# Gate and up of a feed-forward in seven block products of half the tokens

## The chip, the cores and the metric

The kernel runs on one core of one Trainium2 chip. The metric is the time on the device in microseconds (us), the median of several runs. Before the change it is 3476.19 us (3 runs, 3475.81 to 3477.26). A core has five engines with instruction queues of their own: TensorE (PE; its weight loads are PEld in the profile), VectorE (DVE), ScalarE (ACT), GpSimd (POOL) and SyncE (SP). In this kernel SP issues the weight transfers, and the engines wait for one another on semaphores.

## The reference, cut to what matters

All is float32. There are 512 tokens of width 1024, and six feed-forwards (f0 to f5) among attention and recurrent stages. Each feed-forward is

```python
def swiglu(h, w_gu, w_down):                       # f0, f1
    g, u = jnp.split(h @ w_gu, 2, axis=-1)
    return (jax.nn.silu(g) * u) @ w_down

def swiglu_2(x, w_gate, w_up, w_down):             # f2 to f5
    return (jax.nn.silu(x @ w_gate) * (x @ w_up)) @ w_down
```

with an inner width of 2816. `h @ w` for gate and up is a 512 x 1024 by 1024 x 2816 product each.

## The kernel before, in words

Precision. TensorE multiplies numbers rounded to a shorter float32 format (fp32r). Every operand is therefore split in two parts, a main part (rounded, by ScalarE: `hi`, L1145 to L1152) and a lower part (what the rounding left, by VectorE: `lo`, L1649, or `rest`, L1679), and `mm3` (L625 to L627) makes each product of three matmuls: main x main, main x lower, lower x main.

Weights. `weight_units` lists 1 MB units in the order of use; for a feed-forward these are g0, u0, g1, u1, ... g10, u10 (256 columns of gate or up, all 1024 rows: 8 chunks of 128 rows, k = 0 to 7), then d0, d2, ... d20 (rows of the down projection). SP loads them in that order into `STG`, which has three places (`NSTG`); a load waits until `hi` and `lo` of the unit three before have read the place (L445 to L450). ScalarE and VectorE write both parts into `WR`, with three slots (`NWR`); `hi` waits until TensorE has used the unit three before. `after(name)` on ScalarE and VectorE splits the unit three behind `name`.

Feed-forward. On TensorE, `ffn` (L937) makes 22 features of 128 rows for gate and for up; i counts the 11 blocks of 256 columns. Block 0 goes through `first_feats` (L657), which computes each feature in two halves of 256 tokens while the stage before still delivers tokens; blocks 1 to 10 go through `feat` (L641): 8 chunks k of 3 matmuls over all 512 tokens, into one PSUM bank `P`. ScalarE (L1390) applies SiLU to each gate feature (into `XN`), and VectorE (L1990) multiplies it by the up feature into `ACTS`, a view of `BIG`. `prepare(k)` splits an activation for the down projection: into `RB` for k < 4, else over the tokens `HT`, which are free by then. `out_proj` (L732) makes the down projection in groups of two k. `norm_tile` adds and normalizes, and `turn` transposes the result into `HT`.

Order. Each engine's program is written out in the order of its queue, and an instruction that waits holds up all behind it on its engine. GpSimd loads the gains of the norms into `BC` by its own DMA queue (`gain`), and makes a few lower parts outside the feed-forwards.

## Time and profile before

| what | value |
|---|---|
| median of 3 runs | 3476.19 us (3475.81 to 3477.26) |
| span of the profiled execution | 3473.2 us |
| median less span (start and end around the span, and run to run) | 3.0 us |
| PE busy | 3447.0 us, 99% |
| DVE busy | 1442.7 us, 42% |
| ACT busy | 1184.1 us, 34% |
| POOL busy | 154.3 us, 4% |
| chain that ended last | PE 96%, DVE 2%, ACT 2% |
| HBM read | 320.82 MB, 93 GB/s over the span |

No time of its own is given for the profiled execution beside its span. The busy time of PE counts matmuls from start to a modelled end, and neighbours overlap, so the distance between starts tells more than busy time does. The stage f0 runs from about 432 us (its block 0, halves) over 446.5 us (block 1 begins) and 664 us (last up feature) to about 790 us; the other five feed-forwards repeat it.

### The profile page before, as it was taken

To read this page: it belongs to the slowest core of one execution; us is meant where nothing else is said; L and a number is where in the kernel's file an instruction comes from. 1 tells how busy PE (TensorE), PEld (TensorE's weight loads), DVE (VectorE), ACT (ScalarE), POOL (GpSimd) and SP (SyncE) were. 2 spreads that over 40 slices of the span, in tenths; PEclk is the share of its full clock that TensorE was granted. 3 is DMA by queue.
4 is the path that set the end of the run, shared out by engine and by line. 5 is a ranking of instruction groups with operands and counts; after the bars stand their busy time and mean duration, and the time that the engine had idled before them with its cause. 6 is when DMAs were issued, how large, how long until landed. Compare 5 with 4: busy or idle time off the path is not lost.

```text
span 3473.2 us, 39367 instructions
## 1 busy us (share of the span) xinstructions
PE 3447.0 (99%) x17361; PEld 2904.9 (84%) x17361; DVE 1442.7 (42%) x1555; ACT 1184.1 (34%) x1754; POOL 154.3 (4%) x133
## 2 busy tenths in 40 slices
PE   9999999999999999999999999999999999999999
PEld 7788888888888888888888888888888888888887
DVE  4554523337744333332336554223422355552333
ACT  3343422236734222232224343222322233532222
POOL 2110000000000000000000220000000000410000
PEclk9999999999999999999999999999999999999999
DMA  5224232222342322233222203222322223023221
GB/s 155 86 78 140 72 110 97 97 79 92 121 146 66 105 96 95 94 109 97 97 97 77 80 28 106 97 97 97 101 97 96 98 78 112 25 73 101 95 99 57
DMA packets 246477, 325.49 MB, mean 94 GB/s; under 512 B 19361, under 2 KB 215505, under 8 KB 246306
## 3 DMA queue, kind: packets, MB, share of 16 engines
q1 hardware_dynamic: 241520, 308.38, 27.1%
q0 software_dynamic: 4784, 14.59, 1.3%
q8 instruction: 136, 2.23, 0.3%
q14 instruction: 35, 0.29, 0.0%
q10 hardware_dynamic: 2, 0.00, 0.0%
HBM read 320.82 MB, written 2.10 MB: 93 GB/s over the span
## 4 chain that ended last, share of the span: by engine, by line
PE 96%; DVE 2%; ACT 2%; issue 0%; POOL 0%; DMA 0%; DVEq 0%; ACTq 0%
PE P L625 28%; PE P L627 28%; PE P L626 28%; PE P L630 3%; PE P L804 3%; PE P L779 3%; PE P L906 1%; DVE BIG L1662 1%; DVE WR L1654 0%; PE P L907 0%; ACT WR L1152 0%; DVE HT L1662 0%; PE P L1081 0%; PE P L783 0%; PE P L1064 0%; DVE STAT L1789 0%
## 5 line engine op out<-in xcount | busy, mean ns | idle before, releaser
L1654 DVE TENSOR_TENSOR WR<-STG,WR 128x2048 fp32r<-128x2048 f32 (+3 forms) x292 | 646.8, 2217 | 1297.5 <-ACT WR L1152 1297.3
L625 PE MATMUL P<-HT,WR 128*128 128x512 f32 (+1 forms) x3008 | 1119.6, 372 | 3.8 <-DVE HT L1662 2.7
L626 PE MATMUL P<-HT,WR 128*128 128x512 f32 (+1 forms) x3008 | 1116.7, 371 | 0.0
L627 PE MATMUL P<-HT,WR 128*128 128x512 f32 (+1 forms) x3008 | 1116.5, 371 | 0.0
L1152 ACT CAST WR<-STG 128x2048 fp32r<-128x2048 f32 (+3 forms) x324 | 558.8, 1726 | 1066.0 <-PE P L627 1065.4
L625 PEld LDWEIGHTS P<-HT,WR 128*128 128x128 f32 x3008 | 567.4, 189 | 102.0 <-DVE HT L1662 3.0
L627 PEld LDWEIGHTS P<-HT,WR 128*128 128x128 f32 x3008 | 567.5, 189 | 97.3
L626 PEld LDWEIGHTS P<-HT,WR 128*128 128x128 f32 x3008 | 567.6, 189 | 96.8
L625 PE MATMUL P<-WR,HT 128*128 128x512 f32 (+1 forms) x1344 | 523.9, 390 | 1.6 <-DVE WR L1654 1.4
L627 PE MATMUL P<-WR,HT 128*128 128x512 f32 (+1 forms) x1344 | 520.7, 387 | 0.0
L626 PE MATMUL P<-WR,HT 128*128 128x512 f32 (+1 forms) x1344 | 520.3, 387 | 0.0
L625 PEld LDWEIGHTS P<-WR,HT 128*128 128x128 f32 x1344 | 252.4, 188 | 51.7 <-DVE WR L1654 2.2
L627 PEld LDWEIGHTS P<-WR,HT 128*128 128x128 f32 x1344 | 252.3, 188 | 50.3
L626 PEld LDWEIGHTS P<-WR,HT 128*128 128x128 f32 x1344 | 252.5, 188 | 49.0
L1165 ACT ACTIVATE XN<-P 128x512 f32<-128x512 f32 (+1 forms) x156 | 101.5, 652 | 554.4 <-PE P L627 554.4
L1671 DVE SCALAR_TENSOR_TENSOR BIG<-XN,P 128x512 f32<-128x512 f32 x132 | 90.7, 687 | 341.5 <-PE P L627 341.5
L804 PE MATMUL P<-BIG,XN 128*128 128x96 f32 (+2 forms) x928 | 137.3, 286 | 2.1 <-DVE XN L1674 2.1
L1789 DVE TENSOR_REDUCE STAT<-P 128x1 f32<-128x512 f32 (+4 forms) x142 | 84.0, 592 | 117.6 <-PE P L783 84.0
L1165 ACT ACTIVATE BC<-P,STAT 128x256 f32<-128x256 f32 (+3 forms) x192 | 99.1, 520 | 85.6 <-DVE STAT L1789 85.6
L804 PEld LDWEIGHTS P<-BIG,XN 128*128 128x128 f32 x928 | 119.8, 192 | 5.2 <-DVE XN L1674 3.1
L625 PE MATMUL P<-WR,RB 128*128 128x512 f32 (+1 forms) x352 | 116.8, 345 | 0.0
L627 PE MATMUL P<-WR,RB 128*128 128x512 f32 (+1 forms) x352 | 116.2, 343 | 0.0
(204 smaller groups left out, 2413.5 us busy)
## 6 DMA issues: line engine op xcount, KB each, us to landing
STG<-in_w_ffn_gu_dram SPq DMA_DIRECT2D x44, 1024.0 KB, 5.1
STG<-in_ffn_w_gate_dram SPq DMA_DIRECT2D x44, 1024.0 KB, 5.1
STG<-in_ffn_w_up_dram SPq DMA_DIRECT2D x44, 1024.0 KB, 5.1
STG<-in_ffn_w_down_dram SPq DMA_DIRECT2D x44, 1024.0 KB, 4.9
STG<-in_w_ffn_down_dram SPq DMA_DIRECT2D x22, 1024.0 KB, 4.9
STG<-in_w_xkv_dram SPq DMA_DIRECT2D x16, 1024.0 KB, 5.3
STG<-in_w_in_dram SPq DMA_DIRECT2D x12, 1024.0 KB, 5.2
STG<-in_w_xq_dram SPq DMA_DIRECT2D x8, 1024.0 KB, 5.2
```

Of the source, the lines that this page charges most:

```text
L625: pe.matmul(o, lh, rh, start=first, stop=False)
L626: pe.matmul(o, lh, rl, start=False, stop=False)
L627: return pe.matmul(o, ll, rh, start=False, stop=last)
L630: return pe.transpose(o, i, IDENT[0:n, 0:n])
L779: last = pe.matmul(P[:, b, n * kx:(n + 1) * kx], l, r, start=j == 0, stop=j == len(qk) - 1 and a["diag"] is None)
L804: last = pe.matmul(o, PTB[j0 % NP][:, c:c + 128], c_["v"][n][j], start=j == 0, stop=j == nj - 1)
L906: pe.matmul(both, w[0][:, k, 128 * j:128 * j + 128], MT[:, :, k, :], start=k == 0, stop=False)
L1152: a.copy(main, src).then_inc(ac.sem, ac.up("hi", n, *((part,) if part < of - 1 else ())))
L1165: a.activation(o, i, f, **kw).then_inc(ac.sem, ac.up(*point))
L1654: v.tensor_tensor(rests, src, main.bitcast(F32), ALU.subtract).then_inc(ve.sem, ve.up("lo", n))
L1671: v.scalar_tensor_tensor(out=o, in0=x, scalar=s, in1=y, op0=op0, op1=op1).then_inc(ve.sem, ve.up(*point))
L1789: v.tensor_reduce(STAT[:, 80 + h:80 + h + nh], P[:, where[s, "s", i], 0:nh * kx].rearrange("p (h n) -> p h n", h=nh), AX.X, ALU.max, negat ...
```

## The change

Blocks 2 to 10 (`FIRST`, `LAST`) of every feed-forward are computed by another algorithm. Gate and up of a block, each in two halves of the rows k (0 to 3, 4 to 7), times the tokens in two halves (0 to 255, 256 to 511), is a 2 x 2 by 2 x 2 block product. It is made of seven block products in place of eight, with sums of operands. With g', g'' and u', u'' for the row halves:

- sums of weights, per block: S1 = u' + u'' (GpSimd, into `BC`), S3 = g' - u' (over u' in the stage), S2 = S1 - g' (over g'), S4 = g'' - S2 (over g'') (VectorE).
- sums of tokens, once per feed-forward: T5, T7, T6, T4 (VectorE, eight operations of 1024 wide; then split into main and lower part like the weights).
- products p: 1 = g' with the first tokens, 2 = g'' with the first tokens, 3 = S4, 4 = u'' with T4, 5 = S1 with T5, 6 = S2 with T6, 7 = S3 with T7. Each is 2 x 4 x 3 = 24 matmuls of 256 tokens, of operands of 128 x 1024 in main and lower part.
- Between products the sums in PSUM are read: ScalarE copies them after products 1, 6 and 7 (`kept`) before the next product adds to the same place, VectorE adds the other half (`up`, `gate`), ScalarE applies SiLU to a whole pair, and VectorE multiplies.

In steady state the order on TensorE is (i,6) (i,5) (i,7) (i+1,1) (i,4) (i+1,2) (i,3). `WR` becomes a ring of five half slots (`NFORM`) of formed operands; after product e ends, ScalarE makes the main part for product e+5 and VectorE its lower part. The loads of gate i and up i wait for the lower parts of (i-2,3) and (i-2,4); a fourth stage place is laid over `XN`. The places of the activations for the down projection are renumbered (`slot_pair`, `slot_room`), d0, d2 and d4 are split at new points, and GpSimd loads the gains of the norm behind the feed-forward after the lower part of (10,5), not at its start.

The diff, cut to its core:

```diff
+FIRST, LAST = 2, 10
+def products():
+    order = [(FIRST, 1), (FIRST, 2)]
+    for i in range(FIRST, LAST + 1):
+        order += [(i, 6), (i, 5), (i, 7)] + [(i + 1, 1)] * (i < LAST) + [(i, 4)] + [(i + 1, 2)] * (i < LAST) + [(i, 3)]
+    return order
+NFORM = 5
...
+        def stage_free(n):
...
+            if m is not None and m == 3:
+                return [ve.at(s, "act", 2 * FIRST - 1)]
+            if m is not None and m >= 4:
+                return [ve.at(s, "form", PLACE[i - 2, 3 if part == "g" else 4])]
...
+        def form(s, e):
+            return form_slot(s, (e + 3) % NFORM)
+        def form_free(s, e):
+            return mm.at(s, "form", e - NFORM) if e >= NFORM else mm.at("w", U[s, "g", 0] + (1, 1, 2, 3, 3)[e])
...
GpSimd:
+            def ffn(s):
+                for i in range(FIRST, LAST + 1):
+                    up = U[s, "u", i]
+                    g.wait_ge(*landed[stage_of(up)].at("unit", up))
+                    g.wait_ge(*(ve.at(s, "form", PLACE[i - 2, 5]) if i >= FIRST + 2 else ve.at(s, "T32", 4)))
+                    po.tensor_tensor(BC[:, i % 2, :], staged(up)[:, 0:1024], staged(up)[:, 1024:2048],
+                                     ALU.add).then_inc(pl.sem, pl.up(s, "S1", i))
...
TensorE, ffn:
-                for i in range(11):
+                for i in range(FIRST):
...
+                for e, (i, p) in enumerate(PRODUCTS):
+                    sums, rest = 4 * (i % 2), 4 * (i % 2) + 2
...
+                    if p == 6:
+                        g.wait_ge(*ac.at(s, "kept", i, 1))
+                    if p == 7:
+                        g.wait_ge(*ac.at(s, "kept", i, 6))
+                    if p == 4:
+                        g.wait_ge(*ac.at(s, "kept", i, 7))
+                    if p == 3:
+                        g.wait_ge(*ve.at(s, "up", i))
...
+                    g.wait_ge(*ve.at(s, "form", e))
...
+                        for k in range(4):
+                            lh, ll = (z[:, k, 128 * j:128 * j + 128] for z in w)
+                            pe.matmul(o, lh, x[0][:, k], start=k == 0 and p in (1, 2, 5), stop=False, skip_group_check=True)
+                            pe.matmul(o, lh, x[1][:, k], start=False, stop=False, skip_group_check=True)
+                            last = pe.matmul(o, ll, x[0][:, k], start=False, stop=k == 3, skip_group_check=True)
...
ScalarE, ffn:
+                for e, (i, p) in enumerate(PRODUCTS):
...
+                    if p in (1, 6, 7):
+                        g.wait_ge(*mm.at(s, "form", e))
+                        if p == 7:
+                            g.wait_ge(*ve.at(s, "act", 2 * i - 1))
+                        a.copy(UP2 if p == 7 else pair[:, :, 0:256] if p == 1 else pair[:, :, 256:512], sums).then_inc(
+                            ac.sem, ac.up(s, "kept", i, p))
+                    if e + NFORM < len(PRODUCTS):
+                        main(e + NFORM)
+                    if p == 3:
+                        g.wait_ge(*ve.at(s, "gate", i))
+                        fn(pair, pair, ACT.Silu, s, "silu", i)
...
VectorE, ffn:
+                token_sums()
+                after((s, "g", 0))
...
+                for e, (i, p) in enumerate(PRODUCTS):
...
+                    if p == 7:
+                        g.wait_ge(*mm.at(s, "form", e))
+                        g.wait_ge(*ac.at(s, "kept", i, 7))
+                        tt(UP2, UP2, P[:, others:others + 2, 256:512], ALU.add, s, "up", i)
+                    if p == 3:
+                        g.wait_ge(*mm.at(s, "form", e))
+                        tt(pair, pair, P[:, others:others + 2, :], ALU.add, s, "gate", i)
+                    if e + NFORM < len(PRODUCTS):
+                        rests(e + NFORM)
+                    if p == 3:
+                        g.wait_ge(*ac.at(s, "silu", i))
+                        stt(pair[:, :, 0:256], pair[:, :, 0:256], scale, P[:, sums:sums + 2, 0:256], ALU.mult, ALU.mult)
+                        stt(pair[:, :, 256:512], pair[:, :, 256:512], scale, UP2, ALU.mult, ALU.mult, s, "act", 2 * i)
...
+                        i_, p_ = PRODUCTS[e + NFORM]
+                        if p_ == 1:
+                            s1_s3(i_)
+                        if p_ == 4 and i_ < LAST:
+                            s2(i_ + 1)
+                        if p_ == 3 and i_ < LAST:
+                            s4(i_ + 1)
```

`s1_s3(i)` waits for GpSimd's S1 and makes S3; `s2` and `s4` make S2 and S4; `rests(e)` makes a lower part and `main(e)` a main part.

## Rows read from the trace of the kernel before

**Rows 1.** The page: busy time (share of the span), and the chain by engine.

```profile
PE 3447.0 (99%) x17361; PEld 2904.9 (84%) x17361; DVE 1442.7 (42%) x1555; ACT 1184.1 (34%) x1754; POOL 154.3 (4%) x133
...
PE 96%; DVE 2%; ACT 2%; issue 0%; POOL 0%; DMA 0%; DVEq 0%; ACTq 0%
```

**Rows 2.** Waits of PE: who waited <- for whom: us in total, times, longest.

```profile
PE P L625 <- DVE HT L1662: 2.7, 1, 2.7
```

**Rows 3.** PE in order of time: start us, duration us, line, shape.

```profile
438.07 0.28 PE L625 MATMUL P<-HT,WR 128*128 128x256 f32 x1
438.19 0.28 PE L626 MATMUL P<-HT,WR 128*128 128x256 f32 x1
...
450.46 0.39 PE L625 MATMUL P<-HT,WR 128*128 128x512 f32 x1
450.68 0.39 PE L626 MATMUL P<-HT,WR 128*128 128x512 f32 x1
...
```

**Rows 4.** ACT in order of time: SiLUs behind half-width, then full-width features.

```profile
437.91 0.60 ACT L1165 ACTIVATE XN<-P 128x512 f32<-128x512 f32 x1 [2.01 <-PE P L627]
440.79 0.60 ACT L1165 ACTIVATE XN<-P 128x512 f32<-128x512 f32 x1 [2.28 <-PE P L627]
441.28 1.89 ACT L1152 CAST WR<-STG 128x2048 fp32r<-128x2048 f32 x1
...
452.02 0.60 ACT L1165 ACTIVATE XN<-P 128x512 f32<-128x512 f32 x1 [3.50 <-PE P L627]
457.46 0.60 ACT L1165 ACTIVATE XN<-P 128x512 f32<-128x512 f32 x1 [4.84 <-PE P L627]
```

**Rows 5.** Stretches: length, busy PE, PEld, DVE, ACT, POOL (starts); clock; DMA share, GB/s.

```profile
432.00:446.50 14.50, 14.50 (x123) 14.50 (x122) 6.47 (x5) 6.87 (x7) 0.00 (x0) 1.00 0.38 127
446.50:457.40 10.90, 10.90 (x50) 9.00 (x49) 2.98 (x2) 2.51 (x2) 0.00 (x0) 1.00 0.59 192
```

**Rows 6.** DVE groups by form: busy us, mean ns, idle before.

```profile
L1671 DVE SCALAR_TENSOR_TENSOR BIG<-XN,P 128x512 f32<-128x512 f32 x132 | 90.7, 687 | 341.5 <-PE P L627 341.5
...
L1654 DVE TENSOR_TENSOR WR<-STG,WR 128x1024 fp32r<-128x1024 f32 x10 | 12.2, 1223 | 13.9 <-ACT WR L1152 13.9
```

**Rows 7.** DVE in order of time, in f0 and at the end of n0.

```profile
443.21 2.29 DVE L1654 TENSOR_TENSOR WR<-STG,WR 128x2048 fp32r<-128x2048 f32 x1 [6.28 <-ACT WR L1152]
445.42 0.68 DVE L1671 SCALAR_TENSOR_TENSOR BIG<-XN,P 128x512 f32<-128x512 f32 x1
...
2063.23 0.41 DVE L1662 TENSOR_TENSOR HT<-BIG,HT 128x256 fp32r<-128x256 f32 x1
```

**Rows 8.** ACT groups by form: busy us, mean ns, idle before.

```profile
L1165 ACT ACTIVATE XN<-X 128x1024 f32<-128x1024 f32 x20 | 21.2, 1061 | 24.3 <-DVE X L1662 22.2 <-DMA X<-in_x_dram 1.9
...
L1246 ACT COPY XN<-P 128x512 f32<-128x512 f32 x30 | 17.6, 586 | 22.0 <-PE P L630 20.9 <-DVE HT L1662 0.8
...
L1152 ACT CAST WR<-STG 128x1024 fp32r<-128x1024 f32 x10 | 10.5, 1048 | 0.0
```

**Rows 9.** POOL groups, same columns.

```profile
L507 POOL TENSOR_TENSOR HT<-BIG,HT 96x1024 fp32r<-96x1024 f32 x6 | 14.2, 2363 | 0.5
```

**Rows 10.** DMA: landing times of four weight loads; one busy slice; two loads together.

```profile
DMA to landing us min/median/max: 5.0/5.1/5.6
...
449.00:450.00 1.00, 1.00 (x6) 0.81 (x5) 1.00 (x1) 0.00 (x0) 0.00 (x0) 1.00 0.98 340
...
792.21 0.37 SPq L450 DMA_DIRECT2D STG<-in_c_w_in_dram  x1
...
BC<-in_mem_dram POOLq DMA_DIRECT2D x1, 1024.0 KB, 7.5
```

**Rows 11.** POOL in order of time: a load it issued, and two adds.

```profile
793.62 0.72 POOL L550 DMA_DIRECT2D BC<-in_mem_dram  x1 [363.55 <-DVE XN L1671]
...
2046.03 1.82 POOL L494 TENSOR_TENSOR BIG<-BIG 128x768 f32<-128x768 f32 x1 [1.30 <-DVE BIG L1662]
...
2063.39 1.96 POOL L494 TENSOR_TENSOR BIG<-BIG 128x768 f32<-128x768 f32 x1 [4.07 <-DVE BIG L1662]
```

More of the change, by code:

```diff
@@ L263, in build, with raw, stage_of @@
         U = {u[0]: n for n, u in enumerate(units)}
+        downs = [U[f"f{l}", "d", 0] for l in range(6)]
+        slot_of = lambda n: (n - sum(n >= d for d in downs)) % NWR
+        def raw(n):
+            s, part, i = (*units[n][0], 0)[:3]
+            return 2 * (i - FIRST) + (part == "u") if s[0] == "f" and s != "fox" and part in ("g", "u") and i >= FIRST else None
+        def stage_of(n):
+            m = raw(n)
+            if m is None:
+                return slot_of(n)
+            return NSTG if m % 4 == 3 else slot_of(U[units[n][0][0], "g", 0] + 4 + m % 4)
@@ new lines, in staged @@
+        def staged(n):
+            q = stage_of(n)
+            return XN[:, :, :].rearrange("p a n -> p (a n)") if q == NSTG else STG[:, q, :]
+        def stage_free(n):
+            s, part, i = (*units[n][0], 0)[:3]
+            m = raw(n)
+            if m is not None and m == 3:
+                return [ve.at(s, "act", 2 * FIRST - 1)]
+            if m is not None and m >= 4:
+                return [ve.at(s, "form", PLACE[i - 2, 3 if part == "g" else 4])]
+            if m is not None:
+                n0 = U[s, "g", 0] + 1 + m
+                return [ac.at("hi", n0), low(n0)]
+            if n in downs or n - 1 in downs or n - 2 in downs:
+                s = units[n][0][0]
+                last = ((LAST - 1, 3), (LAST, 3), (LAST, 4))[i // 2]
+                return [ve.at(s, "form", PLACE[last])]
+            return [ac.at("hi", n - NSTG), low(n - NSTG)]
@@ new lines, in slot_free, with form_slot @@
+        def slot_free(n):
+            if n in downs or n - 1 in downs or n - 2 in downs:
+                s, _, k0 = units[n][0]
+                return mm.at(s, "form", len(PRODUCTS) - 1 - (3, 1, 0)[k0 // 2])
+            return mm.at("w", n - NWR)
+        def form_slot(s, h):
+            n0 = U[s, "g", 0]
+            q, half = ((n0 + 2, 0), (n0, 0), (n0, 1), (n0 + 1, 0), (n0 + 1, 1), (n0 + 2, 1))[h]
+            return [WR[:, slot_of(n0 + (q - n0)), z, 1024 * half:1024 * half + 1024] for z in range(2)]
@@ new lines, in ffn @@
+                gate(0)
+                after((s, "g", 0))
+                tokens(5)
+                tokens(6)
+                main(0)
+                main(1)
+                gate(1)
+                tokens(7)
+                main(2)
+                main(3)
+                main(4)
+                tokens(4)
+                for e, (i, p) in enumerate(PRODUCTS):
+                    sums = P[:, 4 * (i % 2):4 * (i % 2) + 2, 0:256]
+                    pair = ACTS[:, 2 * i:2 * i + 2, :]
+                    if p in (1, 6, 7):
[9 more added lines that the diff above has]
+                        fn(pair, pair, ACT.Silu, s, "silu", i)
+                    if (i, p) == (LAST, 2):
+                        for k in range(4):
+                            prepare(k)
+                    if (i, p) == (LAST, 7):
+                        hi(U[s, "d", 0])
+                        for k in range(4, 8):
+                            prepare(k)
@@ new lines, in token_sums @@
+                def token_sums():
+                    first, second, up_first, up_second = T32
+                    g.wait_ge(*ve.now())
+                    quadrant(0, 1)
+                    quadrant(1, 4)
+                    g.wait_ge(*ve.now())
+                    tt(first, second, first, ALU.subtract, s, "T32", 5)
+                    quadrant(3, 3)
+                    g.wait_ge(*ve.now())
+                    tt(second, up_second, second, ALU.subtract, s, "T32", 7)
+                    g.wait_ge(*ve.now())
+                    tt(up_second, up_second, first, ALU.subtract, s, "T32", 6)
+                    quadrant(2, 2)
+                    g.wait_ge(*ve.now())
+                    tt(up_first, up_first, up_second, ALU.subtract, s, "T32", 4)
@@ new lines, in tokens, with s1_s3 @@
+                def tokens(p):
+                    main, rests = tokens_of(s, p)
+                    g.wait_ge(*ac.at(s, "T", p))
+                    rest(rests, T32[{5: 0, 7: 1, 4: 2, 6: 3}[p]], main, s, "T", p)
+                def s1_s3(i):
+                    gate, up = U[s, "g", i], U[s, "u", i]
+                    low_ = staged(up)[:, 0:1024]
+                    g.wait_ge(*landed[stage_of(gate)].at("unit", gate))
+                    g.wait_ge(*pl.at(s, "S1", i))
+                    tt(low_, staged(gate)[:, 0:1024], low_, ALU.subtract, s, "S3", i)
@@ new lines, in rests @@
+                def rests(e):
+                    i, p = PRODUCTS[e]
+                    main, rests_ = form(s, e)
+                    g.wait_ge(*ac.at(s, "form", e))
+                    rest(rests_, weights_of(s, i, p), main, s, "form", e)
+                token_sums()
+                after((s, "g", 0))
+                activated(0)
+                tokens(5)
+                tokens(6)
+                s1_s3(FIRST)
+                rests(0)
+                s2(FIRST)
+                rests(1)
```

190 lines of the change are left out of this document (131 added, 59 removed).

## The prediction

> **What bounds the kernel now.** I read the page first: busy shares and the chain that ended last [rows 1]. TensorE is busy for 99% of the span, 96% of the chain is TensorE, and VectorE and ScalarE are at 42% and 34%. The list of who waited for whom [rows 2] says that none of this is hidden idleness: the longest entry of TensorE's waits is 2.7 us in a span of 3473.2. So a change pays by taking TensorE time away, and costs by whatever it newly makes TensorE wait for. Then TensorE's own order of time [rows 3] gives the price of a matmul as the distance between starts, not as its duration (0.28 and 0.39 us, which overlap). Full-width matmuls (512 tokens) start every 0.227 us, half-width ones (256 tokens) every 0.120 us. The SiLUs that follow the feature groups repeat this over 24 matmuls [rows 4]: 437.91 to 440.79 is 2.88 us for 24 half-width matmuls, 452.02 to 457.46 is 5.44 us for 24 full-width ones. The table of stretches [rows 5] shows the half-width rate held for 14.5 us (123 starts, 118 ns each) at granted clock 1.00, the upper level of 2.4 GHz, and the same clock in the full-width stretch behind it.
>
> **The change: what it takes from TensorE.** One weight block (gate and up, 256 columns each) costs 4 features of 24 full-width matmuls now, 4 x 5.44 = 21.76 us. In seven products it costs 7 x 24 half-width matmuls, 7 x 2.88 = 20.16 us. An eighth of the multiplications goes, but half of that is lost again, because a half-width matmul costs 0.120 and not 0.1135. The difference, 1.60 us, comes 9 times (blocks 2 to 10) in each of 6 feed-forwards: 54 x 1.60 = **86.4 us off**. The order per matmul triple and the kinds of operands are those of the half-width rows, so I take no other price.
>
> The Trainium skill, "TensorE: Matmul & The Clock Gate", section "Back-to-back issue gap", gives the isolated gap as N/2.4 + 2.5 ns. By that a block would cost 96 x 215.8 ns = 20.7 us now and 168 x 109.2 ns = 18.3 us after, 128 us off in all. The trace disagrees (227 and 120 ns), and the row decides.
>
> **What it adds on the other engines, per block.** VectorE: seven lower parts and three sums of weights, ten operations of 1024 at 1.223; the gate sum out of PSUM, 1024 wide, at the same; the up sum and two products of 512 at 0.687 [rows 6]. That is 12.23 + 1.22 + 2.06 = 15.5 us against 2 lower parts of 2.29 [rows 7] and 2 products of 0.687, 5.95 us, now. ScalarE: seven casts of 1024 at 1.048, three copies out of PSUM at 0.586, one SiLU of 1024, for which the nearest row is a 1024 activation at 1.061 [rows 8]: 10.2 us. GpSimd: one sum of 1024, 2.36 us by the nearest row, of 96 partitions [rows 9]. All of these fit beside 20.16 us of TensorE: VectorE 77%, ScalarE 51%, GpSimd 12%. So none is the bound by its sum; what can bind is their order.
>
> **The path through the order.** I walked the queues with these durations, 0.05 us a handoff (a cast ends at 441.28 + 1.89 = 443.17, VectorE starts at 443.21, [rows 4, 7]). VectorE's next instruction starts some 0.07 us before the last one's recorded end (443.21 + 2.29 = 445.50, the next at 445.42, [rows 7]), so a 1024 operation occupies 1.15. Formed weights are five products (14.4 us) deep in the ring, so product e+5 is prepared when e ends, with four products (11.5 us) to do 1.05 + 1.22 us in. That cover is wide. VectorE's work is bunched, though: from the end of product 2 of the next block over products 3, 6 and 5 it has about 9.5 us to do without a gap. In that bunch stands the gate sum, behind which ScalarE, in order, has the SiLU and then the copy of product 6, and product 7 waits for that copy. If the gate sum is about 1 us later than in my walk, TensorE stands.
>
> What can make it late is a loop over two loads. Gate i may land only when the lower part for product 3 of block i-2 is made (the end of that bunch). SP issues gate i and up i one behind the other, each 1 MB. GpSimd adds up i's halves. VectorE's S3, at the head of the next bunch, waits for that sum, and the whole bunch is queued behind it. A load alone lands after 5.1 us [rows 10]. Two in a row do not occur on SP's queue in the steady part. Lower bound: the second MB behind the first at the rate of a busy slice, 1.05 MB at 340 GB/s [rows 10], 3.1 and with ramps 3.15, so 5.1 + 3.15 = 8.25 us. Upper bound: an SP load at 792.2 with a 1 MB load from GpSimd's queue at 793.6 that landed 7.5 later, 8.9 us in all [rows 10, 11]. Loop: 8.25 + 0.05 + 2.37 (GpSimd) + 9.46 (VectorE: lower part, S3, gate sum, lower part, two products, S2, two lower parts) + 0.15 (SP) = **20.28 us** against TensorE's 20.16. That is nearly a tie; a loop of 20.5 or more costs about 7 turns of the excess, less 1 us of slack, per feed-forward.
>
> The loop holds GpSimd and a VectorE operation one after the other. The trace has one place that hints at this: the 768-wide GpSimd add that starts at 2063.39 inside a two-input VectorE operation (2063.23 to 2063.64) takes 1.96, where the one at 2046.03 takes 1.82 [rows 7, 11]. If the two run side by side instead, one operation falls out of the loop and it is 19.1 us, with no cost.
>
> The Trainium skill, "SBUF — State Buffer", section "Who interferes with whom", says that a VectorE instruction with two SBUF inputs and a GpSimd instruction that reads SBUF exclude each other for a whole instruction, whoever starts first. By it the loop is 20.3, without it 19.1; the small lengthening in the row agrees, but is too small to prove a full block.
>
> Cost of the loop: lower end 0 (19.1; nothing waited for now, so no gain to win), upper end 7 x (20.93 - 20.16) - 1 = 4.4 us per feed-forward. I take a loop of 20.5, nearer to SP's own queue than to the mixed pair: 7 x 0.34 - 1 = 1.4 us, **8.4 us in all**.
>
> **The ends of each feed-forward.** Start: eight operations for sums of tokens (9.8 us) stand on VectorE ahead of the lower part of up 1, which was made at 443.2 to 445.5 [rows 7] and is needed at 457.4 [rows 4]; even if all 9.8 add to it, 2 us are left. Up 3 loads only after the activation of block 1; its sum is ready about 9 us into the products, and VectorE's next parts wait behind it, but product (2,4), the first that needs one, starts at 17.3: hidden, with 6 us left. End: in block 10 product 4 follows 7 with no product of a next block between them, so the copy of product 7 is bare: 0.16 until the last matmul has drained (0.28 less 0.12) + 0.59 + 0.1 for two handoffs = 0.85 us, six times, **5.1 us**. The first down units (ready 3 us ahead) and the last activations (2 us ahead) are covered. Moved gain loads on GpSimd's queue come before the down phase, some 100 us before use: nothing. The other stages keep their instructions: nothing. DMA bytes do not change.
>
> **Sum.** 86.4 - 8.4 - 5.1 = 72.9 us. The profiled span 3473.2 becomes 3400.3. The median of the runs, 3476.19, lies 3.0 us above the span (what lies around it, plus run to run, 1.5 us); it is unchanged: **3403 us**.
>
> **Rivals.**
> (a) The loop binds in earnest: second landing at 8.9 and a GpSimd sum lengthened by one VectorE operation beside it to about 2.8, loop 21.3. Loss 7 x 1.14 - 1 = 7 us per feed-forward, 42 us in place of 8.4: 3437. For it: a loop without slack, a price of GpSimd known only beside idle VectorE. Against it: the SP queue's landings are even (5.0 to 5.6, [rows 10]).
> (b) Slower than before: the GpSimd sum falls into VectorE's bunch, they stop each other, and the sum takes 5.5 us. The loop is then 23.4, the loss 7 x 3.25 - 1 = 21.8 and 0.9 at the end, against 14.4 won per feed-forward: +8.3 x 6 = 50, 3526. The point from which it decides: a loop of 22.2 us, which is a GpSimd sum of 4.3 us. Against it: the only lengthening seen is 0.14. The Trainium skill names the mechanism ("SBUF — State Buffer", section "Who interferes with whom": "the other fully blocks"), not such a duration.
> (c) The loop does not bind, 19.1 to 20.3, nothing but 5.1 is lost: 3395.
> (d) It does not do what it says: half-width matmuls with a wait every 24 run at the rate per column of full ones or worse. At 0.1295 us each a block costs 21.76 and all is gone: 3482. The rows speak against it [rows 3 to 5], since groups of 24 with waits between them already keep 2.88.
>
> **Chances.** Forecast (3398 to 3412) 0.46; (c) 0.20; (a), from 3412 to 3465, 0.22; (b) 0.06, (d) and a loop that eats just the gain 0.06, two thirds of it within 0.2%. 0.2% (7 us) is about what a measurement of this kernel can tell from no change. Faster by more: 0.88; within: 0.04; slower: 0.08. Range: 3390 (rival (c) with the 5.1 not all bare) to 3445 (rival (a) with a bit more); what lies outside is (b), (d) and the far part of (a), under 0.2.
>
> **What would show it.** Product groups at 2.88 us, seven to a block, show the first step; anything longer at granted clock 1.00 refutes it. TensorE's waits should be on ScalarE's copies: six of 0.85 before product 4 of block 10, and small ones before product 7 of a block, fewer than 0.4 each. The distance between issues of gate loads shows the loop: 20.2 to 20.5. GpSimd's sum at 2.4 shows that the exclusion is cheap, at 3 or over it is rival (a), at 4.3 or over (b). Landing of the up load more than 8.5 after the gate issue also goes to (a). The prediction is wrong if TensorE waits for formed weights, or if the ends of the feed-forwards show waits that I held for hidden.

## The result, and the profile after

The changed kernel takes 3396.94 us (median of 4 runs, 3395.53 to 3397.53) beside 3476.65 us for the kernel before on the same chip: a ratio of 0.9771, 95% interval 0.9757 to 0.9784, 79.7 us less. The forecast was 3403 in a range of 3390 to 3445. The profiled execution has a span of 3395.7 us, the granted clock is 1.00.

The page of the changed kernel: busy time, the chain that ended last, and three groups (busy us, mean ns, idle before), to be read beside [rows 1, 6, 8].

```profile
span 3395.7 us, 48396 instructions
PE 3364.8 (99%) x21249; PEld 3021.7 (89%) x21249; DVE 2048.6 (60%) x2167; ACT 1465.9 (43%) x2156; POOL 299.9 (9%) x187
...
PE 90%; DVE 4%; issue 3%; ACT 2%; POOL 1%; DMA 1%; SPq 0%; DVEq 0%; ACTq 0%; POOLq 0%
...
L1096 PE MATMUL P<-HT,WR 128*128 128x256 f32 x1728 | 489.6, 283 | 4.1 <-ACT CUM L1595 4.1
...
L1851 DVE TENSOR_TENSOR WR<-STG,WR 128x1024 fp32r<-128x1024 f32 x276 | 378.3, 1384 | 112.8 <-ACT WR L1574 112.6
...
L1574 ACT CAST WR<-STG 128x1024 fp32r<-128x1024 f32 x276 | 287.7, 1050 | 204.9 <-PE P L1098 186.4
```

TensorE has 3888 more matmuls and is still busy for 99%. VectorE went from 1442.7 to 2048.6 us, ScalarE from 1184.1 to 1465.9, GpSimd from 154.3 to 299.9, and none of them is near the span. The casts cost what they were priced at (1050 ns), but the 276 of the 378 lower parts in the group shown average 1384 ns and not 1223: the first hint that something stretches VectorE's operations.

TensorE's waits in the changed kernel (who <- for whom: us in total, times, longest), beside [rows 2]:

```profile
PE P L1096 <- ACT CUM L1595: 4.1, 6, 0.7
PE P L748 <- DVE XN L1860: 3.1, 2, 1.6
```

The first entry is new, one in each feed-forward: the copy after product 7 of block 10. In order of time (start us, duration us, and in brackets the idle time before and its cause), the copy and the matmuls behind it:

```profile
645.92 0.59 ACT L1595 COPY CUM<-P 128x512 f32<-128x512 f32 x1 [4.05 <-PE P L1098]
```

```profile
646.56 0.39 PE L1096 MATMUL P<-HT,WR 128*128 128x256 f32 x1 [0.68 <-ACT CUM L1595]
646.78 0.28 PE L1097 MATMUL P<-HT,WR 128*128 128x256 f32 x1
```

The start before 646.56 is 0.96 us earlier, 0.84 more than the usual 0.12, and the next one follows after 0.22 in place of 0.12: 0.93 us in all, before rounding.

I measured the stretch of the 63 products in each feed-forward as the distance from its first matmul's start to its last (1512 starts), and 0.12 us for the last matmul itself. Without a wait it would be 63 x 2.88 = 181.44 us.

| feed-forward | stretch, us | over 181.44 | made of |
|---|---|---|---|
| f0, f1, f4, f5 | 182.37 each (f4, f5 182.36) | 0.93 | the copy after product 7 |
| f2 | 182.72 | 1.28 | the same, and one wait of 0.35 at 1656.20 |
| f3 | 183.42 | 1.98 | the same, and three of 0.35 at 2151.43, 2212.25, 2273.08 |

The sum is 6.96 us: 5.6 for the copies, 1.4 for the four small waits, all four before a product 7. So 54 x 1.60 - 6.96 = 79.4 us should be gained, and 79.7 was by the medians. (The two profiled spans differ by 77.5; the changed kernel's is of the slowest of its four runs.) That leaves the four small waits to explain, and the loop, which was forecast at 8.4 and cost 1.4.

The turn of the loop (from one issue of a gate load to the next) before the wait at 2151.43, in the changed kernel: POOL's sum, then VectorE, then ScalarE.

```profile
2143.90 3.45 POOL L664 TENSOR_TENSOR BC<-STG 128x1024 f32<-128x1024 f32 x1 [15.25 <-DMA STG<-in_ffn_w_up_dram]
```

```profile
2143.86 1.23 DVE L1851 TENSOR_TENSOR WR<-STG,WR 128x1024 fp32r<-128x1024 f32 x1 [1.71 <-ACT WR L1574]
2147.45 1.23 DVE L1851 TENSOR_TENSOR STG<-STG 128x1024 f32<-128x1024 f32 x1 [2.36 <-POOL BC L664]
2148.59 1.21 DVE L1851 TENSOR_TENSOR BIG<-BIG,P 128x1024 f32<-128x1024 f32 x1
```

```profile
2149.84 1.06 ACT L1313 ACTIVATE BIG<-BIG 128x1024 f32<-128x1024 f32 x1 [3.13 <-DVE BIG L1851]
2150.81 0.57 ACT L1595 COPY BIG<-P 128x512 f32<-128x512 f32 x1
```

The sum starts 0.04 us behind a VectorE lower part, and takes 3.45 us where 42 of the 54 sums take 2.39 to 2.42. VectorE stands for 2.36 us on it; S3, the gate sum, the SiLU and the copy of product 6 follow without a gap, the copy ends at 2151.38, and product 7 starts at 2151.43. This is the path that the prediction drew, with a sum 1.05 longer.

In the next turn it is the other way round. SP's gate loads, POOL's sum, then VectorE's lower part and S3:

```profile
2155.66 0.37 SPq L560 DMA_DIRECT2D STG<-in_ffn_w_gate_dram  x1
2175.46 0.37 SPq L560 DMA_DIRECT2D STG<-in_ffn_w_gate_dram  x1
```

```profile
2163.86 2.40 POOL L664 TENSOR_TENSOR BC<-XN 128x1024 f32<-128x1024 f32 x1 [16.52 <-DMA XN<-in_ffn_w_up_dram]
```

```profile
2164.37 2.98 DVE L1851 TENSOR_TENSOR WR<-STG,WR 128x1024 fp32r<-128x1024 f32 x1 [1.71 <-ACT WR L1574]
2167.27 1.21 DVE L1851 TENSOR_TENSOR XN<-STG,XN 128x1024 f32<-128x1024 f32 x1
```

The sum is first and keeps its 2.40 us (to 2166.26). The lower part, begun 0.51 us behind it, takes 2.98 us and ends 1.09 behind the sum's end, so S3 starts 1.01 behind it in place of the 0.10 above. Of the 42 turns (blocks 4 to 10 of six feed-forwards) 38 go like this one. In the other four the sum is stretched, and these are the four before the small waits; the up load had landed late in all of them, 9.29 to 9.61 us after the gate issue.

From one gate issue to the next it is 19.72 to 21.33 us, 20.24 on average over 36 distances. Each is the landing of the up load (7.95 to 9.67 us after the gate issue, in 13 of the 42 turns 9.22 or more) plus 11.65 to 12.05. So a turn with a late landing is longer than TensorE's 20.16, most of the others are shorter, and the lead that is lost in one (how far the copy of product 6 is ready ahead of product 7) is won back in the next. Why every third landing or so is late, no run here shows. Product 7 starts 3.98 us behind the start of S3 where it waits, and 4.11 to 5.74 behind it in the 38 turns where it does not.

### The profile page after: what moved, and what is told of

The parts are those of the page before. It is cut to its first block, busy times and chain, and to the rows that moved or that the text cites. A ratio compares the mean times of both kernels' runs of the same rounds, so it can differ in the third digit from the quotient of the medians.

```text
span 3395.7 us, 48396 instructions
## 1 busy us (share of the span) xinstructions
PE 3364.8 (99%) x21249; PEld 3021.7 (89%) x21249; DVE 2048.6 (60%) x2167; ACT 1465.9 (43%) x2156; POOL 299.9 (9%) x187
## 3 DMA queue, kind: packets, MB, share of 16 engines
q8 instruction: 167, 2.74, 0.3%
## 4 chain that ended last, share of the span: by engine, by line
PE 90%; DVE 4%; issue 3%; ACT 2%; POOL 1%; DMA 1%; SPq 0%; DVEq 0%; ACTq 0%; POOLq 0%
PE P L743 17%; PE P L745 17%; PE P L744 17%; PE P L1096 9%; PE P L1098 9%; PE P L1097 9%; PE P L921 3%; PE P L748 3%; PE P L896 3%; DVE BIG L1851 1%; PE P L1023 1%; POOL BC L664 1%; DMA STG<-in_ffn_w_up_dram 1%; DVE WR L1843 1%; PE P L1024 0%
## 5 line engine op out<-in xcount | busy, mean ns | idle before, releaser
L1843 DVE TENSOR_TENSOR WR<-STG,WR 128x2048 fp32r<-128x2048 f32 (+3 forms) x184 | 398.5, 2172 | 643.0 <-ACT WR L1300 642.8
L1300 ACT CAST WR<-STG 128x2048 fp32r<-128x2048 f32 (+4 forms) x216 | 352.4, 1637 | 564.6 <-PE P L745 563.8
L1096 PE MATMUL P<-HT,WR 128*128 128x256 f32 x1728 | 489.6, 283 | 4.1 <-ACT CUM L1595 4.1
L1098 PE MATMUL P<-HT,WR 128*128 128x256 f32 x1728 | 489.1, 283 | 0.0
L1097 PE MATMUL P<-HT,WR 128*128 128x256 f32 x1728 | 489.0, 283 | 0.0
L743 PE MATMUL P<-WR,HT 128*128 128x512 f32 (+1 forms) x1248 | 485.7, 389 | 1.6 <-DVE WR L1843 1.4
L745 PE MATMUL P<-WR,HT 128*128 128x512 f32 (+1 forms) x1248 | 483.3, 387 | 0.0
L744 PE MATMUL P<-WR,HT 128*128 128x512 f32 (+1 forms) x1248 | 483.0, 387 | 0.0
L743 PE MATMUL P<-HT,WR 128*128 128x512 f32 (+1 forms) x1280 | 447.8, 350 | 2.7 <-DVE HT L1851 1.6
L1851 DVE TENSOR_TENSOR WR<-STG,WR 128x1024 fp32r<-128x1024 f32 x276 | 378.3, 1384 | 112.8 <-ACT WR L1574 112.6
L744 PE MATMUL P<-HT,WR 128*128 128x512 f32 (+1 forms) x1280 | 444.9, 348 | 0.0
L745 PE MATMUL P<-HT,WR 128*128 128x512 f32 (+1 forms) x1280 | 444.7, 347 | 0.0
L1574 ACT CAST WR<-STG 128x1024 fp32r<-128x1024 f32 x276 | 287.7, 1050 | 204.9 <-PE P L1098 186.4
L1096 PEld LDWEIGHTS P<-HT,WR 128*128 128x128 f32 x1728 | 331.7, 192 | 5.5 <-ACT CUM L1595 5.3
L1097 PEld LDWEIGHTS P<-HT,WR 128*128 128x128 f32 x1728 | 331.7, 192 | 0.2
L1098 PEld LDWEIGHTS P<-HT,WR 128*128 128x128 f32 x1728 | 331.7, 192 | 0.0
L743 PEld LDWEIGHTS P<-WR,HT 128*128 128x128 f32 x1248 | 234.3, 188 | 48.0 <-DVE WR L1843 2.2
L745 PEld LDWEIGHTS P<-WR,HT 128*128 128x128 f32 x1248 | 234.2, 188 | 46.7
L744 PEld LDWEIGHTS P<-WR,HT 128*128 128x128 f32 x1248 | 234.4, 188 | 45.4
L743 PEld LDWEIGHTS P<-HT,WR 128*128 128x128 f32 x1280 | 243.4, 190 | 33.7 <-DVE WR L1843 2.1
L745 PEld LDWEIGHTS P<-HT,WR 128*128 128x128 f32 x1280 | 243.4, 190 | 30.1
L744 PEld LDWEIGHTS P<-HT,WR 128*128 128x128 f32 x1280 | 243.5, 190 | 29.4
```

Source lines behind the costliest of these rows:

```text
L743: pe.matmul(o, lh, rh, start=first, stop=False)
L744: pe.matmul(o, lh, rl, start=False, stop=False)
L745: return pe.matmul(o, ll, rh, start=False, stop=last)
L1096: pe.matmul(o, lh, x[0][:, k], start=k == 0 and p in (1, 2, 5), stop=False, skip_group_check=True)
L1097: pe.matmul(o, lh, x[1][:, k], start=False, stop=False, skip_group_check=True)
L1098: last = pe.matmul(o, ll, x[0][:, k], start=False, stop=k == 3, skip_group_check=True)
```

## The experiments

All times are medians; every kernel but two starts from the changed one (3396.9 us). The kernel before took 3476.65 us beside the changed one and 3475.69 to 3476.05 beside the others, so differences under 1 us in the third column say nothing; the last column, from the traces, is the sharper one.

| kernel | us | against the changed one | product stretches over 181.44 us, six together |
|---|---|---|---|
| changed | 3396.9 | | 7.0 |
| sum on VectorE | 3394.8 | -2.1 | 5.6 |
| up load first | 3394.7 | -2.3 | 5.6 |
| last block reordered | 3392.4 | -4.6 | 2.4 |
| up load first, last block reordered | 3389.1 | -7.9 | 0.0 |
| sum twice | 3510.6 | +113.7 | 120.1 |
| sum twice, up load first | 3396.3 | -0.7 | 6.6 |
| zeros ahead of the sum | 3420.4 | +23.5 | 29.0 |
| before, half-width features | 3544.7 | (before: 3476.1) | |
| before, quarter-width features | 4616.8 | (before: 3475.7) | |

### The sum on VectorE

```diff
 GpSimd, ffn:
-                    po.tensor_tensor(BC[:, i % 2, :], staged(up)[:, 0:1024], staged(up)[:, 1024:2048],
-                                     ALU.add).then_inc(pl.sem, pl.up(s, "S1", i))
 VectorE, s1_s3:
+                    g.wait_ge(*landed[stage_of(up)].at("unit", up))
+                    tt(BC[:, i % 2, :], low_, staged(up)[:, 1024:2048], ALU.add, s, "S1", i)
```

> The sum S1 = u' + u'' is made by VectorE, just ahead of S3, and GpSimd makes none. Nothing else changes. My theory: the loop over the two loads does not bind in the changed kernel (7 loads in a row are 20.2 us apart, TensorE's period is 20.16), and its four single waits of 0.35 us before product 7 (one in f2, three in f3) come from a GpSimd sum that VectorE's two-input operation stretched to 3.0 to 3.4 us. Then the sum costs 1.15 us on VectorE in place of 2.41 on GpSimd, the loop gets shorter by 1.2 us (to about 18.9), the four waits go, and the time is 3396.9 - 1.4 = 3395.5 (3394.5 to 3397). Rival: what sets product 7's cover is the length of VectorE's bunch (S3, gate sum, lower parts), 9.5 us now and 10.6 with the sum in it; then the copy before product 7 comes late in every block, 54 waits of 0.3 to 1 us, 3413 to 3450.

3394.81 us (3394.13 to 3396.44; ratio to before 0.9767, 0.9753 to 0.9782). All six stretches are 182.37 us: the four waits of 0.35 are gone, only the copies are left, and the 1.15 us more in VectorE's bunch shows nowhere. The rival falls. The runs alone scarcely tell the two kernels apart; of the 2.1 us between the medians 1.4 are in the stretches, and the kernel before was 0.8 us faster beside this one.

### The up load first

```diff
 SyncE:
+            sequence = list(range(len(units)))
+            for n in range(len(units)):
+                m = raw(n)
+                if m is not None and m >= 4 and m % 2 == 0:
+                    sequence[n], sequence[n + 1] = n + 1, n
-            for n, (_, srcs, p, k, w) in enumerate(units):
+            for n in sequence:
```

> For blocks 4 to 10 SP issues the load of up i ahead of the load of gate i, so that it waits only for the lower part of (i-2,4), two products earlier than that of (i-2,3). My theory: GpSimd's sum then starts about 5.8 us earlier relative to VectorE's bunch and is out of the loop, which is left with one load, about 5.2 + 9.5 + 0.2 = 15 us; the four waits of 0.35 go: 3395.5 (3394.5 to 3397). GpSimd's sums may be stretched in other places than now, without a wait of TensorE behind. Rival: the four waits come from the exclusion of the two engines wherever the sum falls; then TensorE waits at new places, as many or more, 3397 to 3410.

3394.66 us (3392.83 to 3395.41; 0.9766, 0.9749 to 0.9782), stretches of 182.36 to 182.37 again. GpSimd's groups in this kernel:

```profile
L670 POOL TENSOR_TENSOR BC<-STG 128x1024 f32<-128x1024 f32 x30 | 100.0, 3333 | 951.4 <-DVE BIG L1857 597.7 <-DMA STG<-in_ffn_w_up_dram 237.6 <-DVE WR L1857 67.2
L670 POOL TENSOR_TENSOR BC<-XN 128x1024 f32<-128x1024 f32 x24 | 73.0, 3043 | 442.0 <-DMA XN<-in_ffn_w_up_dram 280.3 <-DVE WR L1857 82.9 <-DMA XN<-in_w_ffn_gu_dram 78.8
```

45 of the 54 sums are now stretched past 2.6 us (12 in the changed kernel), and yet TensorE waits for none. So a stretched sum costs time only where it stands in the loop. One of them, and VectorE's operations around it:

```profile
502.37 3.37 POOL L670 TENSOR_TENSOR BC<-XN 128x1024 f32<-128x1024 f32 x1 [15.70 <-DVE WR L1857]
```

```profile
502.26 1.22 DVE L1857 TENSOR_TENSOR STG<-STG 128x1024 f32<-128x1024 f32 x1
503.60 0.69 DVE L1857 TENSOR_TENSOR CUM<-CUM,P 128x512 f32<-128x512 f32 x1
504.49 2.34 DVE L1857 TENSOR_TENSOR WR<-STG,WR 128x1024 fp32r<-128x1024 f32 x1 [0.20 <-ACT WR L1580]
```

It is read so. VectorE's operation on two operands in SBUF began at 502.26 and ends at 503.48; GpSimd's, issued at 502.37, lasts until 505.74, 2.3 us behind that end, about what it takes alone. VectorE's next one of this kind starts at 504.49 and takes 2.34 in place of 1.22: it ends 1.1 us behind 505.74. The operation between them, with one operand in SBUF and one in PSUM, runs beside GpSimd's at its ordinary 0.69. Whole instructions exclude each other, in the order of issue. The Trainium skill says just this ("SBUF — State Buffer", section "Who interferes with whom"), and the trace agrees in both orders and in the exemption of the PSUM operand.

### The last block reordered, and both together

```diff
-    for i in range(FIRST, LAST + 1):
-        order += [(i, 6), (i, 5), (i, 7)] + [(i + 1, 1)] * (i < LAST) + [(i, 4)] + [(i + 1, 2)] * (i < LAST) + [(i, 3)]
+    for i in range(FIRST, LAST):
+        order += [(i, 6), (i, 5), (i, 7), (i + 1, 1), (i, 4)] + [(i + 1, 2)] * (i < LAST - 1) + [(i, 3)]
+    order += [(LAST, p) for p in (6, 2, 7, 5, 4, 3)]
```

The weight sum S4 of block 10 moves behind the lower part for (10,2). The up sum of block 10 moves from product (10,7) to (10,5), and with it on VectorE the first split for the down projection and the lower parts of activations 4 to 7; on ScalarE the main parts of these activations move too.

> Only the order of the last block's products is changed: (10,2) goes from before (9,3) to behind (10,6), and (10,5) goes behind (10,7), so that the copy after product 6 and that after product 7 each have a product between them and the product that adds to the same place; the sum of the up halves moves with (10,5). My theory: the bare copy after product 7 of block 10 costs 0.93 us in each feed-forward and nothing else takes its place: 3396.9 - 5.6 = 3391.3 (3390.3 to 3392.5). Rival: the time is only moved, since the split of the first down unit and the first activations lie behind that copy and are then late by as much; 3396 to 3398, with a wait of 0.5 to 0.9 us at the first product of the down projection.

3392.39 us (3391.92 to 3392.68; 0.976, 0.9745 to 0.9774). The six waits of 0.93 are gone and nothing takes their place at the end; f1 and f5 are 181.44 and 181.43 us long, the ideal. But there are now seven of the small waits of 0.35 before product 7 (one in f0 and f4, two in f2, three in f3), 2.4 us instead of 1.4. That is nearly all of the 1.1 us by which the expectation was missed. Again they are just the turns (seven of 42) in which the sum was issued behind the start of the lower part and was the one to be stretched. Which of the two comes first changes with everything that shifts a landing.

> Both: up loads ahead of gate loads, and the last block's order as in the run above. If both theories hold the gains add: 1.4 + 5.6 = 7.0 us, 3389.9 (3389 to 3391.5), and the product stages of all six feed-forwards are 63 products x 2.88 = 181.4 us long, with no wait over 0.1 us on TensorE in them. Otherwise it shows the wait that is left.

3389.09 us (3388.21 to 3390.92; 0.9751, 0.9736 to 0.9765), 7.9 less than the changed kernel. All six stretches are 181.43 or 181.44 us, and no matmul in them starts more than 0.3 us after the last one. Its list of waits no longer names a product; the longest entry is now one that the kernel before has too (L779 there, 2.5 us in 6):

```profile
PE P L903 <- DVE BIG L1859: 2.5, 6, 0.5
```

This is the best version: the 86.4 us of the first step, whole.

### The sum twice, with the loads in either order

```diff
 GpSimd, ffn:
+                    po.tensor_tensor(BC[:, i % 2, :], staged(up)[:, 0:1024], staged(up)[:, 1024:2048],
+                                     ALU.add).then_inc(pl.sem, pl.up())
+                    g.wait_ge(*pl.now())
                     po.tensor_tensor(BC[:, i % 2, :], staged(up)[:, 0:1024], staged(up)[:, 1024:2048],
                                      ALU.add).then_inc(pl.sem, pl.up(s, "S1", i))
```

> GpSimd makes its sum twice, the second time over the first, and only the second lets the others go on: the sum takes 4.9 us in place of 2.4. The theory of the prediction: landing of up 8.1 us after the gate issue, then sum, then VectorE's 9.5 us, one after the other, 8.1 + 4.9 + 9.5 + 0.3 = 22.8 us against TensorE's 20.16; if GpSimd and VectorE's two-input operations also stop each other, the loss is about 16.5 us per feed-forward, 3396.9 + 99 = 3496 (3475 to 3515); if the sum runs beside VectorE at no cost to either, about 9 us each, 3451 (3440 to 3465). Rival: the sum is hidden behind TensorE with several us of room, and the prediction's loop is not there at all: 3397 to 3403.

> The doubled sum again (4.9 us), but with up i loaded ahead of gate i, so that the sum is out of the loop. If the loop is what makes a long sum dear, it costs next to nothing here: 3398 (3395 to 3404), against about 3496 with the loads in their old order. Rival: a long GpSimd sum is dear because it stops VectorE itself, wherever it falls; then VectorE's bunch is longer by up to 2.4 us here as well, and most of the loss is still there: 3440 or more.

3510.62 us (3510.03 to 3511.22; 1.0099, 1.007 to 1.0128) with the loads as they were, slower than the kernel before; 3396.26 us (3395.86 to 3396.66; 0.977, 0.9742 to 0.9798) with the up load first. The same doubled sums cost 114 us in the one. In the other they cost a wait of 1.07 us in f3, and 1.6 us beside the up load first alone (3394.66). The loop is real, and the way out of it is the order of two loads. The chain that ended last, in order of time, shows one whole turn of the loop in the first of the two (start us, us, what):

```profile
553.07 0.37 SPq L560
...
553.48 7.63 DMA XN<-in_w_ffn_gu_dram
...
561.17 2.44 POOL BC L664
...
563.69 3.27 POOL BC L667
...
567.06 1.23 DVE XN L1854
568.28 1.13 DVE BIG L1854
569.41 1.13 DVE WR L1854
570.55 1.28 DVE BIG L1863 x2
571.83 1.14 DVE STG L1854
572.97 2.28 DVE WR L1854 x2
575.27 0.37 SPq L560
```

From 553.07 to 575.25 there is not a TensorE instruction in it: SP issues gate (0.37), then up, which lands 7.63 us later; two sums, the second stretched to 3.27; then VectorE for 8.19 us (S3, gate sum, lower part, two products, S2, two lower parts), and SP again. The other turns differ in the landing (7.6 to 9.2) and in the stretch. Between sums that start a turn lie 22.4 to 22.8 us on average.

The expectation of 3496 was 15 us short. The waits account for only part of the 120.1 us: 48 of them, 84.4 us in all, 5.0 of it the six copies. The other 36 us are matmuls that start late: only the second one behind a wait, by 0.1 us, 28 times, and whole runs of them, 33 us. Behind a wait of 2.74 us, in this kernel:

```profile
500.54 0.28 PE L1101 MATMUL P<-RB,WR 128*128 128x256 f32 x1
503.40 0.38 PE L1099 MATMUL P<-WR 128*128 128x256 f32 x1 [2.59 <-ACT BIG L1598]
...
504.19 0.41 PE L1101 MATMUL P<-WR 128*128 128x256 f32 x1
504.40 0.41 PE L1099 MATMUL P<-WR 128*128 128x256 f32 x1
504.62 0.41 PE L1100 MATMUL P<-WR 128*128 128x256 f32 x1
```

and the table of stretches (length, busy PE and starts, granted clock, DMA share, GB/s) around it:

```profile
496.00:500.00 4.00, 4.00 (x36) 1.00 0.02 4
504.00:508.00 4.00, 4.00 (x24) 0.58 0.00 0
508.00:512.00 4.00, 4.00 (x36) 1.00 0.82 262
```

The matmuls start 0.21 us apart for a while, the granted clock of those 4 us is 0.58, so most of them ran at the lower level of 1.2 GHz, and by 508 it is back at 2.4 GHz. Of the 28 waits of 1.90 us or longer in this kernel, 20 were followed by 13 to 27 such matmuls, 1.4 to 2.7 us lost; of the 20 of 1.12 us or shorter none was. The waits alone, with 0.1 behind each, would have given 3396.9 - 7.0 + 84.4 + 4.8 = 3479, 3 us above the kernel before; the other 31 us are the clock.

### Zeros ahead of the sum

```diff
 GpSimd, ffn:
+                    po.memset(BC[:, i % 2, :], 0.0).then_inc(pl.sem, pl.up())
+                    g.wait_ge(*pl.now())
```

> As the changed kernel, but GpSimd first writes zeros over the place of its sum (1024 wide; the row 128x512 took 0.525, so about 0.95 with a handoff of 0.1), then makes the sum. The loop gets 1.05 us longer and nothing else is added: a price for a small excess, where the doubled sum gave that of a large one (22.5 us, 3510.6). Theory: the loop without it is 20.3, with GpSimd and VectorE stopping each other; with it 21.3, seven turns of 1.15 less 1 us of slack, 7 us per feed-forward, 3396.9 + 40 = 3437 (3430 to 3446), waits of TensorE before product 7 of about 1 us, at full clock throughout. This is the rival (a) of the prediction made on purpose. Rival: the sum and VectorE's operation run side by side, the loop has 1.2 us of room, and the zeros cost nothing: 3397 to 3399.

3420.43 us (3419.12 to 3421.85; 0.984, 0.9823 to 0.9856). Both numbers of the expectation are wrong, 3437 as well as the rival's 3397: the zeros do cost, but 3.7 us per feed-forward and not 7. The chain goes through the loop in this kernel too. Two turns of it:

```profile
567.50 0.37 SPq L560
...
567.91 7.69 DMA STG<-in_w_ffn_gu_dram
...
575.65 0.95 POOL BC L664
...
576.68 3.02 POOL BC L666
...
588.01 0.37 SPq L560
...
588.42 8.97 DMA XN<-in_w_ffn_gu_dram
...
597.45 0.95 POOL BC L664
...
598.48 2.41 POOL BC L666
```

The first turn is 20.51 us (567.50 to 588.01), the second 21.2; VectorE is in both for 8.2 us behind the sum. The second is the plain loop: landing 9.38 after the gate issue, zeros with their handoff 1.03, sum 2.41, VectorE 8.2, other handoffs 0.16. The first by the same terms, with its landing of 8.10 and a sum of 2.4, would be 19.9 us, below TensorE's 20.16; its sum is stretched to 3.02. That is why the excess cost little: only late landings make the plain loop long, and the six turns of a feed-forward are 20.72 on average, 6 x 0.56 = 3.4 of the 3.9 us over the copy.

It also shows where the 0.35 comes from. In all 42 turns of this kernel the lower part comes ahead of the sum, as in four of the changed kernel; the zeros, issued first, do not hold it up. 20 of the 36 turns on that chain are 20.50 to 20.52 us long, with landings from 7.67 to 8.08 us: GpSimd's part, zeros and sum, is the longer the earlier the load lands (3.99 for 7.68, 3.59 for 8.08), so that its end does not move, and an earlier landing would not shorten the turn. It ends 2.3 us behind a VectorE lower part, whose own start is tied to the end of a product (at 576.21 in the first turn shown, the sum was issued at 576.68). From that lower part over sum, S3, gate sum, SiLU and copy to product 7 it takes 0.35 us more than TensorE has to do meanwhile. 29 of the 42 waits before product 7 here have this size, like all four in the changed kernel.

### Narrower matmuls in the kernel before

```diff
 TensorE, ffn, blocks 2 to 10, h in range(2) and n 256 wide; in the second kernel range(4) and 128 wide:
-                            feat(w, 128 * j, 128, b, (s, name, f))
+                            for h in range(2):
+                                c, n = slice(128 * j, 128 * j + 128), slice(256 * h, 256 * h + 256)
+                                for k in range(NK):
+                                    last = mm3(P[:, b, n], w[0][:, k, c], w[1][:, k, c], HT[:, 0, k, n], HT[:, 1, k, n],
+                                               k == 0, k == NK - 1)
```

> The kernel before, with each feature of blocks 2 to 10 made in two halves of 256 tokens: the same 96 products of a block in 192 matmuls of half the width, eight half groups where the changed kernel has seven. Nothing else is changed. Theory of the prediction, from rows: a half-width matmul costs 0.120 us against half of 0.227, so a block takes 8 x 2.88 = 23.04 us in place of 21.76, 54 x 1.28 = 69 us more than before: 3545.8 (3540 to 3550). By the Trainium skill, TensorE: Matmul & The Clock Gate, section Back-to-back issue gap, it would be 192 x 109.2 against 96 x 215.8 ns, 54 x 0.25 = 13.5 us more: 3490. Were the half-width matmul itself free of any extra cost: 3476.7.

3544.66 us (3544.63 to 3544.69; 1.0197, 1.0167 to 1.0226): 68.6 us more than before, 69 by the rows. Eight half groups cost 23.04 us where seven cost 20.16, and so the first step of the prediction is shown by itself, on a kernel that has none of the rest of the change. The isolated gap of the Trainium skill ("TensorE: Matmul & The Clock Gate", section "Back-to-back issue gap") gave an estimate of 13.5 us more, and the measured 68.6 does not agree; the section itself says that a stream of weight loads and matmuls has another pace.

> The kernel before with each feature of blocks 2 to 10 made in four quarters of 128 tokens (384 matmuls of a block, a quarter of the width). It asks what the extra cost of a narrow matmul is. Full width costs 227 ns, half width 120: both are columns / 2.4 plus 13.5 ns. If that is a fixed cost per matmul, a quarter costs 53.3 + 13.5 = 66.8 ns, a block 25.7 us against 21.76, 54 x 3.9 = 211 us more: 3687 (3675 to 3700). Rival: at this width the loading of the 128 x 128 weights ahead of each matmul sets the pace, at any rate between 70 and 120 ns a matmul: 3750 to 4790, at 120 ns (no cheaper than a half-width one) 46.1 us a block, 4790.

4616.80 us (4616.37 to 4617.22; 1.3279, 1.3253 to 1.3306). Both of my single numbers, 3687 and 4790, miss; the time lies in the wide range of the rival (3750 to 4790). A block takes 21.76 + 1141.1 / 54 = 42.9 us, 111.7 ns for a matmul of 128 tokens. In order of time in this kernel:

```profile
599.91 0.28 PE L625 MATMUL P<-HT,WR 128*128 128x128 f32 x1
600.02 0.28 PE L626 MATMUL P<-HT,WR 128*128 128x128 f32 x1
600.13 0.27 PE L627 MATMUL P<-HT,WR 128*128 128x128 f32 x1
```

Halving the width from 256 to 128 saves 8 ns. "Columns / 2.4 plus 13.5 ns" holds for 256 and 512 columns and not below: at 128 something else sets the pace. The load of 128 x 128 weights ahead of each matmul is the same at every width and is the candidate; that it is the load is argued, not shown. The Trainium skill ("TensorE: Matmul & The Clock Gate", section "LDWEIGHTS (loading the stationary operand)") gives P/1.2 for it, an estimate of 106.7 ns for 128 columns, near the 111.7 here.

## Why the prediction was right, point by point

- What bounds the kernel: right. TensorE's time came down by what its own instructions lost, and VectorE at 60% and ScalarE at 43% cost nothing by their load.
- What TensorE gains, 86.4 us from 0.227 and 0.120 us a matmul: right. Four stretches are 63 x 2.88 plus one wait to 0.01 us, and the half-width features alone repeat the price (68.6 for 69). Rival (d) is out. One word is off: of the 2.72 us that an eighth of a block is worth, the width takes back 1.12, two fifths and not half.
- The price of the added instructions: right for the casts (1050 for 1048 ns), the copies (0.57 to 0.59 for 0.586), the SiLU (1.06 for 1.061), and the sum when nothing is in its way (2.40 to 2.41 for 2.37). A lower part alone is 1.22 to 1.23 as priced; the group's mean of 1384 ns holds the 38 that wait for GpSimd's sum, at 1.64 to 3.27.
- The exclusion of GpSimd and VectorE: the prediction left it open between 19.1 and 20.3 us of loop and called the 0.14 us in the rows "too small to prove a full block". It is a full block, in both directions, and it strikes in all 42 turns. In 38 the lower part waits and S3 starts 1.0 us behind the sum, which lengthens the loop by 0.9 without a wait of TensorE; in four the sum waits, and product 7 with it, by 0.35 us. By the rows a turn with a landing of 8.1 to 8.3 would be 18.9 to 19.1 us without the block; these turns were 19.8 to 20.2. The sign that the prediction gave, a sum of 2.4 us, looked at the wrong engine: the sum kept its 2.4 and VectorE paid. Six sums of 4.3 us, by that sign a case for rival (b), are the first of each feed-forward; they stand ahead of the loop, and no product waited.
- The cost of the loop, 8.4 us: this term was mis-sized, it cost 1.4 us. Its parts were nearly right: landing 8.25 for 8.58 on average, sum 2.37 for 2.40, VectorE 9.46 for 9.2 (1.0 from the sum's end to S3 and 8.19 from there), in all 20.28 for 20.24 on average. Wrong was the step from there to the cost. "I take a loop of 20.5" goes up from my own 20.28 towards a row of two different queues; with 20.28 the same formula gives no cost at all. And it makes seven equal turns out of turns of 19.7 to 21.3 us: a single late landing is paid from the lead of product 7, and only in four turns, where the sum also came behind the lower part, was there a wait. "7 turns of the excess" are rather six: with a loop of 22.56 in the doubled sum, 6 x 2.4 - 1 = 13.4, and 13.2 us per feed-forward were waited.
- The ends, 5.1 us: the mechanism and the place were right, the size 5.6. What was missing is the start after the first one, 0.22 in place of 0.12. The hidden parts (sums of tokens, the late up 3, the first down units) were hidden: no wait at any of them, 182.37 is full with the copy.
- The sum: -86.4 + 5.6 + 1.4 = -79.4 instead of -72.9; the forecast of 3403 was 6 us too high, and rival (c), 3395 with a loop that does not bind, was nearer than the forecast itself. The time lies just below the stretch that the forecast was given (3398 to 3412), and well in the range. (c) had 0.20 against 0.46, although my own 20.28 lay inside its 19.1 to 20.3.
- Rival (a) needed a loop of 21.3 in every turn. One of its signs was there, the up load landed more than 8.5 us after the gate issue in 15 of 42 turns, but such turns mostly stood singly; the zeros ahead of the sum, made for it, gave 20.6 to 20.8 and 3420. Rival (b), slower than before through a long sum, was made with the doubled sum: a loop of 22.56, past the 22.2 from which it was to decide, and 3510.6. Its formula gives 6 x (7 x 2.4 - 1 + 0.9 - 14.4) = +14, 3490. That is 11 us more than the waits gave (3479), and the other 31 us to 3510.6 are the clock, which no part of the prediction had.

## What to carry to other kernels

Price a product in smaller blocks by the start-to-start time of matmuls of the new width, from the same kernel: of the eighth saved here two fifths went to the width. When several engines and a load form a loop, add up what each must do after the thing it waits for, with an operation that the other engine shuts out counted in, and compare it with the bound engine's period turn by turn, since a lead covers single long turns and not a long mean. Then break the loop where it is cheap, here by swapping two loads, which made a sum of twice the length free. Keep a short read of PSUM from standing bare between two products of the same place: another product between them was worth 0.93 us each time.

## What the runs showed of the hardware that was not expected

- A half-width matmul (256 columns) starts every 120 ns and a quarter-width one (128) every 111.7: in this stream narrower than 256 buys almost nothing.
- TensorE's clock can be lost inside a kernel that is 97% busy: after 20 of 28 waits of 1.90 us or more the matmuls started 0.21 us apart, 33 us in all on top of 84.4 us of waiting. A loop that binds by 2.4 us a turn therefore cost some 40% more than its waits.
- GpSimd's zeros, which only write SBUF, took 0.95 to 0.96 us in all 54 places, and a VectorE lower part that began inside one (576.21, the zeros from 575.65 to 576.60) kept its 1.22; the sums, which read, took 2.4 to 3.3. The Trainium skill ("SBUF — State Buffer", section "Who interferes with whom") says that a VectorE instruction with two SBUF inputs does not contend with one of GpSimd that only writes SBUF, and these rows agree.
